# Two of nine score products per mixing stage as column sums by a tile of ones

## The reference

```python
b = jnp.cumsum(gc, axis=2)
inter = jnp.einsum('bhck,bhkv->bhcv', qc * jnp.exp(b), state)
diff = b[:, :, :, None, :] - b[:, :, None, :, :]
decay = jnp.exp(jnp.where(tril[:, :, None], diff, -jnp.inf))
scores = jnp.einsum('bhtk,bhsk,bhtsk->bhts', qc, kc, decay)
intra = jnp.einsum('bhts,bhsv->bhtv', scores, vc)
```

## Time and profile before

| what | value |
|---|---|
| median of 3 runs | 1738.81 us (1738.01 to 1739.43) |
| profiled execution: time / span | 1739.63 us / 1737.8 us |
| granted PE clock, mean | 0.999 of 2.4 GHz |
| busy share of the span: PE / DVE / ACT / POOL | 99% / 72% / 57% / 3% |
| chain that ended last, share of PE | 90% |

### The profile page before, as it was taken

The page is one execution under the profiler, slowest core; times in us unless marked ns, Lnnn a source line. Parts: engine busy times, 40 slices in busy tenths (PEclk is TensorE's granted clock), DMA queues, the critical chain, the costliest instruction groups (busy, mean ns, idle before and its releaser), DMA issues.

```text
span 1737.8 us, 24185 instructions
## 1 busy us (share of the span) xinstructions
PE 1725.9 (99%) x9517; PEld 1498.4 (86%) x9517; DVE 1252.2 (72%) x1584; ACT 998.8 (57%) x1247; POOL 59.3 (3%) x95
## 2 busy tenths in 40 slices
PE   9999999999999999999999999999999999999998
PEld 8888998888888888888889888888888988888887
DVE  6766777766677566875667898866657898876565
ACT  6544666644467454754457866464446966565454
POOL 7200000000000000000001000000000000000000
PEclk9999999999999999999999999999999999999999
DMA  7765535665655655465545554356565554445652
GB/s 244 240 194 185 177 122 169 217 216 180 206 169 176 206 186 188 141 199 192 193 147 191 186 167 145 122 185 218 178 209 169 164 176 134 138 165 194 200 187 96
DMA packets 211564, 311.65 MB, mean 179 GB/s; under 512 B 6434, under 2 KB 166112, under 8 KB 211360
## 3 DMA queue, kind: packets, MB, share of 16 engines
q1 hardware_dynamic: 207472, 303.84, 53.4%
q0 software_dynamic: 3712, 6.44, 1.3%
q10 hardware_dynamic: 304, 0.33, 0.1%
HBM read 309.54 MB, written 1.05 MB: 179 GB/s over the span
## 4 chain that ended last, share of the span: by engine, by line
PE 90%; ACT 5%; DVE 3%; issue 2%; DMA 0%; SPq 0%; ACTq 0%; DVEq 0%
PE psD L1968 28%; PE psA L1905 20%; PE psA L1912 11%; PE psA L1826 7%; PE psA L1831 3%; PE psA L1935 3%; PE psA L1950 3%; PE psA L1770 3%; PE psA L1968 2%; PE psD L2253 2%; ACT hi L454 2%; PE psA L1954 1%; PE psA L1939 1%; PE psA L1775 1%; PE psA L2038 1%
## 5 line engine op out<-in xcount | busy, mean ns | idle before, releaser
L926 DVE TENSOR_TENSOR lo<-raw,hi 128x2048 fp32r<-128x2048 f32 x285 | 650.6, 2290 | 120.1 <-ACT hi L454 119.4
L454 ACT ACTIVATE hi<-raw 128x2048 fp32r<-128x2048 f32 x285 | 542.9, 1911 | 62.2 <-PE psD L1968 33.5
L1905 PE MATMUL psA<-xT,hi 128*128 128x512 f32 x1536 | 355.9, 389 | 0.0
L1905 PEld LDWEIGHTS psA<-xT,hi 128*128 128x128 f32 x1536 | 288.3, 188 | 59.8
L1968 PE MATMUL psD<-hi,prod_hi 128*128 128x512 f32 x544 | 213.5, 392 | 0.2 <-DVE prod_lo L1303 0.2
L1968 PE MATMUL psD<-hi,prod_lo 128*128 128x512 f32 x544 | 212.6, 391 | 0.0
L592 ACT ACTIVATE scr<-psA 128x512 f32<-128x512 f32 x66 | 39.4, 597 | 296.5 <-PE psA L1912 278.7
L1912 PEld LDWEIGHTS psA<-xT,lo 128*128 128x128 f32 x1536 | 190.6, 192 | 3.7
L1912 PE MATMUL psA<-xT,lo 128*128 128x256 f32 x1536 | 191.8, 283 | 0.0
L1284 DVE TENSOR_TENSOR scr<-psA,scr 128x512 f32<-128x512 f32 x66 | 45.6, 691 | 192.2 <-ACT scr L592 192.2
L1968 PE MATMUL psD<-lo,prod_hi 128*128 128x512 f32 x544 | 143.6, 389 | 0.0
(11 more groups left out here) (311 smaller groups left out, 2155.4 us busy)
## 6 DMA issues: line engine op xcount, KB each, us to landing
raw<-in_w_in SPq DMA_DIRECT2D x48, 1024.0 KB, 5.2
raw<-in_ffn_w_up SPq DMA_DIRECT2D x43, 1024.0 KB, 5.7
raw<-in_ffn_w_gate SPq DMA_DIRECT2D x43, 1024.0 KB, 5.4
raw<-in_ffn_w_down SPq DMA_DIRECT2D x43, 1024.0 KB, 5.0
raw<-in_w_gate SPq DMA_DIRECT2D x22, 1024.0 KB, 5.4
raw<-in_w_up SPq DMA_DIRECT2D x22, 1024.0 KB, 5.6
raw<-in_w_down SPq DMA_DIRECT2D x22, 1024.0 KB, 5.0
raw<-in_lru_w_in SPq DMA_DIRECT2D x10, 1024.0 KB, 5.4
```

The source lines that it names most:

```text
L454: act.activation(hi[:, n % RING, :], raw_of(n), ACT.Copy).then_inc(hi_ready, 1)
L926: dve.tensor_tensor(lo[:, n % RING, :], raw_of(n), hi[:, n % RING, :].bitcast(F32), ALU.subtract).then_inc(lo_ready, 1)
L1905: pe.matmul(psA[:, bank + f, :], w[:, k, f * P:(f + 1) * P], xT[:, k].rearrange("p e s -> p (e s)"), start=(k == 0), stop=False)
```

## The change

The diagonal and the last level (m = 1) no longer use fp32 products. Where only one key per query is wanted, the score is a sum over the 128 key channels (the partitions) of an elementwise product. So the elementwise product is made first, split into a high and a low fp32r part in `prod_hi` and `prod_lo`, and PE multiplies it with a 128x128 tile of ones (`ones_r`): four matmuls of 128x512 for each of the two. Every row of the result holds the same sums; the masks pick what is wanted.

The diagonal: POOL adds the keys and multiplies with the query (both 128x1024), ACT copies to the high part (i = 9), DVE subtracts for the low part (i = 9, behind `exponents(1)`), and PE sums after block 10, in front of `turn_heads(1)`. ACT copies the result into `near` at i = 11; `cross` is copied at i = 10.

The last level: `exponents(7)` makes only the query's two subtractions, `level(7)` exponentiates half as much, `scaled(7)` makes the elementwise products, ACT copies to the high part at i = 23 (behind the split of block 25), DVE subtracts for the low part at i = 23, and PE sums between the two token tiles of block 23. In layer 0 `exponents(0)` moves from i = 7 to i = 5.

```diff
+        ones_r = sb("ones_r", [P, P], F32R)
...
+                if kind == "mix":
+                    l, HS = stage[1], HEADS * S
+                    pool.wait_ge(kk_ready, 2 * l + 2)
+                    pool.tensor_tensor(view(K_SUM, HS), view(KK, HS), view(KK + HS, HS), ALU.add).then_inc(diag_summed, 1)
+                    pool.wait_ge(diag_summed, l + 1)
+                    pool.wait_ge(query_evac, 2 * l + 2)
+                    pool.tensor_tensor(view(K_SUM, HS), view(K_SUM, HS), view(Q_B, HS), ALU.mult).then_inc(diag_in, 1)
...
-                        act.activation(e2, e2, ACT.Exp).then_inc(decay_out, 1)
+                        v = e2 if LEVELS[i] > 1 else e2[:, 0:HS]
+                        act.activation(v, v, ACT.Exp).then_inc(decay_out, 1)
...
+                    def last_high():
+
+                        act.wait_ge(last_in, l + 1)
+                        act.activation(prod_hi[:].rearrange("p a b s -> p (a b s)"), tmp2[:, HS:2 * HS], ACT.Copy).then_inc(last_hi, 1)
+
+                    def diagonal_high():
+
+                        act.wait_ge(diag_in, l + 1)
+                        act.activation(prod_hi[:].rearrange("p a b s -> p (a b s)"), view(K_SUM, HS), ACT.Copy).then_inc(diag_hi, 1)
...
-                        if i in (E0 + 1, E0 + 3):
-                            take((i - E0 - 3) // 2)
+                        if i == E0 + 2:
+                            diagonal_high()
+                        if i == NP - 1:
+                            last_high()
+                        if i == E0 + 3:
+                            take(0)
+                        if i == E0 + 4:
+                            take(-1)
...
+            settle()
+            dve.tensor_copy(ones_r[:], one_row[:]).then_inc(ones_ready, 1)
...
-                    def diagonal():
-
-                        dve.wait_ge(kk_ready, 2 * l + 2)
-                        settle()
-                        dve.tensor_tensor(view(K_SUM, HS), kk2[:, 0:HS], kk2[:, HS:2 * HS], ALU.add).then_inc(scaled_ready, 1)
+                    def last_low():
+
+                        dve.wait_ge(last_hi, l + 1)
+                        dve.tensor_tensor(prod_lo[:].rearrange("p a b s -> p (a b s)"), tmp2[:, HS:2 * HS],
+                                          prod_hi[:].rearrange("p a b s -> p (a b s)").bitcast(F32), ALU.subtract).then_inc(last_lo, 1)
+
+                    def diagonal_low():
+
+                        dve.wait_ge(diag_hi, l + 1)
+                        dve.tensor_tensor(prod_lo[:].rearrange("p a b s -> p (a b s)"), view(K_SUM, HS),
+                                          prod_hi[:].rearrange("p a b s -> p (a b s)").bitcast(F32), ALU.subtract).then_inc(diag_lo, 1)
...
-                        step(dve.tensor_tensor(ek[:, :, 0, :], f_end, f[:, :, 0, :], ALU.subtract))
-                        step(dve.tensor_tensor(ek[:, :, 1, :], b_end, b[:, :, 1, :], ALU.subtract))
+                        if m > 1:
+                            step(dve.tensor_tensor(ek[:, :, 0, :], f_end, f[:, :, 0, :], ALU.subtract))
+                            step(dve.tensor_tensor(ek[:, :, 1, :], b_end, b[:, :, 1, :], ALU.subtract))
...
+                        if m == 1:
+                            settle()
+                            t_, kf, kb, to = (halves(v, 1) for v in (tmp2[:, 0:HS], kk2[:, 0:HS], kk2[:, HS:2 * HS], tmp2[:, HS:2 * HS]))
+                            step(dve.tensor_tensor(to[:, :, 1, :], t_[:, :, 1, :], kf[:, :, 0, :], ALU.mult))
+                            step(dve.tensor_tensor(to[:, :, 0, :], t_[:, :, 0, :], kb[:, :, 1, :], ALU.mult))
+                            settle()
+                            dve.memset(stat[:, 15:16], 0.0).then_inc(last_in, 1)
+                            return
...
-                            diagonal()
                             if not l:
                                 sums(0)
                                 sums(1)
+                                exponents(0)
...
-                        if (i - E0) % 2 == 0 and l <= (i - E0) // 2 < NL:
+                        if (i - E0) % 2 == 0 and 1 <= (i - E0) // 2 < NL:
                             exponents((i - E0) // 2)
+                        if i == E0 + 2:
+                            diagonal_low()
+                        if i == NP - 1:
+                            last_low()
...
+                    def summed_by_ones():
+
+                        for b in range(2):
+                            for z in (prod_hi, prod_lo):
+                                last = pe.matmul(psD[:, b, :], ones_r[:], z[:, b].rearrange("p a s -> p (a s)"), start=(z is prod_hi), stop=(z is prod_lo))
+                        last.then_inc(pair_done, 1)
...
-                            tokens_last(n + 1, n, (lambda: pair(NL - 1)) if i == NP - 1 else None)
+                            tokens_last(n + 1, n, last_level if i == NP - 1 else None)
...
-                        if (i - E0) % 2 == 0 and 0 <= (i - E0) // 2 < NL:
+                        if (i - E0) % 2 == 0 and 0 < (i - E0) // 2 < NL:
                             pair((i - E0) // 2 - 1)
+                        if i == E0 + 3:
+                            diagonal()
```

More of the change, by code:

```diff
@@ L176, in build @@
         scaled_ready, pair_done, pair_taken = sem("scaled_ready"), sem("pair_done"), sem("pair_taken")
+        diag_summed, diag_in, diag_hi, diag_lo, last_in, last_hi, last_lo, ones_ready = sem("diag_summed"), sem("diag_in"), sem("diag_hi"), sem("diag_lo"), sem("last_in"), sem("last_hi"), sem("last_lo"), sem("ones_ready")
         rec_done, rec_square, rec_sum, rec_rms, rec_ready = sem("rec_done"), sem("rec_square"), sem("rec_sum"), sem("rec_rms"), sem("rec_ready")
@@ L798, in level @@
                             return
-                        act.activation(e2, e2, ACT.Exp).then_inc(decay_out, 1)
+                        v = e2 if LEVELS[i] > 1 else e2[:, 0:HS]
+                        act.activation(v, v, ACT.Exp).then_inc(decay_out, 1)
                     def take(i):
-                        act.wait_ge(pair_done, (NL + 1) * l + i + 2)
+                        act.wait_ge(pair_done, (NL + 1) * l + (2 if i < 0 else 1))
                         act.activation(near if i < 0 else cross, pairs, ACT.Copy).then_inc(pair_taken, 1)
+                    def last_high():
[4 more added lines that the diff above has]
+                        act.activation(prod_hi[:].rearrange("p a b s -> p (a b s)"), view(K_SUM, HS), ACT.Copy).then_inc(diag_hi, 1)
                     def exponentials(u):
@@ L1576, in scaled @@
                         dve.wait_ge(decay_out, (NL + 2 * HEADS + 1) * l + 2 * HEADS + 2 + i)
-                        dve.wait_ge(pair_done, (NL + 1) * l + i + 1)
+                        if i:
+                            dve.wait_ge(pair_done, (NL + 1) * l + (1 if i == 1 else i + 1))
                         step(dve.tensor_tensor(tmp2[:, 0:HS], view(Q_B, HS), e2[:, 0:HS], ALU.mult))
+                        if m == 1:
[6 more added lines that the diff above has]
+                            return
                         ek, kf, kb, to = (halves(v, m) for v in (e2[:, HS:2 * HS], kk2[:, 0:HS], kk2[:, HS:2 * HS], tmp2[:, HS:2 * HS]))
@@ L2238, in _, with last_level, diagonal @@
                     qkT, w_att, wT = view(QK_T, 2, HEADS, S), view(W_ATT, 2, S), view(W_T, 2, T, P)
-                    def pair(i):
[L2242 to L2248, removed]
+                    def last_level():
+                        pe.wait_ge(last_lo, l + 1)
+                        pe.wait_ge(pair_taken, (NL + 1) * l + NL)
+                        summed_by_ones()
+                    def diagonal():
+                        pe.wait_ge(ones_ready, 1)
+                        pe.wait_ge(diag_lo, l + 1)
+                        pe.wait_ge(pair_taken, (NL + 1) * l + 1)
+                        summed_by_ones()
+                    def summed_by_ones():
[3 more added lines that the diff above has]
+                        last.then_inc(pair_done, 1)
+                    def pair(i):
+                        pe.wait_ge(scaled_ready, (NL - 1) * l + i + 1)
+                        if i:
+                            pe.wait_ge(pair_taken, (NL + 1) * l + i + 1)
+                        q, k_ = tmp2[:, 0], tmp2[:, 1]
                         ps = psD[:, 0:2, :].rearrange("p b (e s) -> p (b e) s", s=P)
@@ L2251, in pair @@
                             for e in range(T):
-                                te = 1 - e if i >= 0 and LEVELS[i] == P else e
+                                te = 1 - e if LEVELS[i] == P else e
                                 last = pe.matmul(ps[:, 2 * hh + e, :], k_[:, hh, e * P:(e + 1) * P], q[:, hh, te * P:(te + 1) * P],
```

## The result

| | before | changed |
|---|---|---|
| median | 1738.9 us (6 runs) | 1752.09 us (6 runs, 1751.6 to 1754.28) |
| ratio, with its 95% interval | | 1.008 (1.0068 to 1.0091) |
| profiled execution: time / span | 1739.63 / 1737.8 | 1751.65 / 1749.9 |
| granted PE clock, mean | 0.999 | 0.997 |

What follows compares the result with a forecast made beforehand. PE was taken as the bound nearly everywhere. Layer 0 +1.7 + 2.7 = +4.4 and layer 1 +0.1 + 2.7 = +2.8 made +7.2 us: 1746.0 us against a median of 1738.81, 8-in-10 range 1741.5 to 1749.0.

Steps and rivals of the forecast that it cites:

- saves 0.80: PE's own work: four fp32r matmuls (0.91 us) replace an fp32 product (1.71), 0.80 us each, 3.2 us in all.
- The wait in block 23: Last level, each layer: PE waits 3.5 us for last_low, which is queued behind head_norm on DVE.
- the clock: Rival, chance 0.12: PE's clock drops to 1.2 GHz in both layers' 3.5 us waits, for as long as each; 1749.5 us.
- this term: Block 23, each layer: 3.5 us of wait and 0.91 instead of 1.71 of work make PE 2.7 us later.
- DVE keeps the lock: Rival, chance 0.2: in layer 0 DVE holds POOL off through the scans; layer 0 +2.0, in all +4.9, 1743.7 us.
- No cost from POOL: Rival, chance 0.1: POOL's products don't delay DVE at all; layer 0 +1.6, in all +4.4, 1743.2 us.
- Not slower: Rival, chance 0.13 (or nearly so): last level's sum in time, no wait in block 23; -2.6, 1736.2 us.
- layer 1's head, +0.1: Layer 1, head of the stage: PE reaches turn_heads(1) at 1400.45 instead of 1400.36, the saved product gone.
- the low part of block 7 wants to start at 1371.70 and ends at 1375.9: Layer 1's head: POOL delays this DVE step; PE stalls 0.9 us, costing nothing more since it waits at pair(0) anyway.
- layer 0's head: Layer 0, head of the stage: PE stalls 0.6 and 2.3 us through POOL's products, 1.7 us late at turn_heads(1).

Runs made afterwards that it cites:

- run 6: Changed kernel with block 23's chain one step earlier: scaled(7) before take(6), ACT's copy before its split, last_low before head_norm; 1742.13 us (1.0021).
- run 5: Changed kernel with DVE's head_norm moved from in front of last_low to behind it, at i = 23; 1746.07 us (1.0041).
- run 2: Changed kernel with PE's wait in block 23 filled by fourteen matmuls whose result nobody reads; 1748.83 us (1.0059).
- run 1: Changed kernel with the diagonal's two elementwise products made on DVE and none on POOL; 1748.03 us (1.0056).
- run 3: Changed kernel with only the diagonal as in the change; the last level goes back to fp32 products; 1743.86 us (1.003).
- run 10: Changed kernel as it is, profiled a second time; 1752.48 us (1.0078), profiled span 1751.5.
- run 4: Changed kernel with only the last level as in the change; the diagonal by the old fp32 product, nothing on POOL; 1748.58 us (1.0055).
- run 7: Changed kernel with POOL's two products held back until the low part of block 9 is written; 1754.27 us (1.009).

## Why the forecast was wrong

**Right.** The sum of four matmuls instead of `pair(7)` saves 0.80 (measured 0.82 and 0.86 in run 6). The wait in block 23 is 3.35 us (forecast 3.5), made by `head_norm` in front of `last_low`; run 5 leaves 1.55 of it, for ACT's copy, where I had put 1.8. Without the clock this term is +2.7 per layer, as forecast (run 2). POOL gets its turn in DVE's first gap, so the rival "DVE keeps the lock" falls. "No cost from POOL" falls with run 1. "Not slower" falls with the wait itself: it decided below 1.4 us.

**Wrong, first: layer 1's head, +0.1.** The step that failed is "the low part of block 7 wants to start at 1371.70 and ends at 1375.9". I had counted only DVE's instructions with two input tiles as open to POOL's lock, and so passed over `maximum`, which stands right in front of that low part. It takes 3.9 us longer, and the low part of block 7 ends at 1382.90, 10.21 us behind the start of block 6; the step had it at 8.2. By PE's rows: 2.82 of wait, less the 1.71 of the diagonal's product and the 0.50 of `pair(0)`'s old wait, plus 0.91 of the new sum, is 1.5; run 3 measures 1.74. So 1.6 us of the miss are here. The Trainium skill (SBUF — State Buffer, "Who interferes with whom") would have warned of it: besides the two-input rule that I used, it lists `tensor_scalar` among the instructions that can take the shared ports, if their operands meet certain conditions. The trace agrees, with 2561 ns for one that takes 402 alone.

**Wrong, second: the clock.** It was a rival with a chance of 0.12 at 1749.5. It is the larger part. In the first profile it costs 1.5 to 1.6 us behind each wait of block 23 (99.46 and 99.43 against the 97.85 to 97.95 of runs 2 and 10) and 1.1 in layer 1's head (35.48 against 34.39), 4.2 us together. Three things in my reasoning failed. The sum put the clock at nothing, because no row showed a fall amid dense work. I let it act on block 23 alone, and it also comes behind waits of 2.3 and 2.8 us. And I let it stay down for as long as PE had waited. In all profiles here a low stretch amid the work lasts 3.4 us (fourteen times) or 6.8 (twice), behind a wait of 2.26 us as behind one of 3.36. That half of the 3.5 us wait, 1.75, came near the 1.6 of one fall was luck.

The account for the profiled execution's span: 7.2 forecast, +1.6 for layer 1's head without the clock, +4.2 for the clock, -0.2 for layer 0's head, -0.7 for the start: 12.1, as measured. The medians differ by 13.2, because the old kernel's profiled execution was 0.7 us above its median and the changed kernel's 0.4 below.

**Open.** Why the clock fell behind a wait of 2.26 us in one execution and not behind one of 3.36 us in the same one, no run tells. A rival to the length of the wait, the moment at which it comes in an execution, was not tested. So the changed kernel's time has a spread of its own (1751.6 to 1754.28), which none of its waits has in the two profiles. A version with all POOL and order effects gone and also ACT's evacuation in layer 1 moved was not tried.

## What to carry to other kernels

A saving on the engine that sets the time is worth nothing until the data are there: here 3.2 us of matmuls were saved and 16 us paid, in waits that the order of two other queues and POOL's lock made, and in the slow clock behind them. Price a wait on PE at its own length, and add what the clock may cost behind it: here 1.6 us and more for waits of 2.3 to 3.4 us, in some executions. If the wait can't be removed, useless matmuls in it can be cheaper than idleness (3.3 us here). Before work goes to GpSimd, list every VectorE instruction that it will run beside, those with one tensor input too: here each of POOL's products held one of them back until it ended.

## What the runs showed of the hardware

- A `tensor_scalar` of 128x256, one SBUF input tile and scalars per partition, went from 402 ns to 2159 and 2561 ns while POOL ran a `tensor_tensor`. It ended 0.15 us behind POOL's instruction each time. With POOL's work elsewhere it took 403 to 409 ns (runs 1, 4 and 7).
- A `tensor_tensor` of 128x512 with one input in PSUM and one in SBUF ran beside POOL's sum for 0.48 us (changed kernel, 1373.52 to 1374.20), and neither took longer: 0.69 and 2.41 us.
- DVE and POOL took turns: when both had instructions ready, one instruction of each went through in alternation, however short DVE's was (0.28 us between two that were held back to 2.5 and 2.4, run 7). POOL's product took 2.40 when it got in at once, 4.34 when the low part of block 7 held the lock.
- The granted clock fell to 0.50 at or behind waits of 2.26, 2.81 and 3.35 us amid dense work, in some executions and not in others (seven of the ten unfilled waits of 3.35 to 3.40 us), and not once behind the waits of 1.38 and 1.55 us in the profiles of runs 1 and 5. It stayed there for 3.4 us, or 6.8, whatever the wait. A fall cost 1.6 us in most cases, from 1.1 to 2.7 at the ends (run 4's last rest, 100.67 against 97.95).
